# A third early query tile, weight tiles 9 to 11 in halves, and reordered first attention steps in a two-layer decoder trunk

## The reference, cut to what matters

```python
for l in range(DEPTH):                                   # DEPTH = 2
    mod = (silu(c) @ w_ada[l] + b_ada[l])                # 6 vectors of 2048: sh1, sc1, g1, sh2, sc2, g2
    h = rmsnorm(x, norm_g[l, 0]) * (1.0 + sc1) + sh1
    proj = h @ w_in[l]                                   # u | q | kc vc | ks vs | kw vw | gate logits
    a_out = pool_mixer(u, w_pool[l], pool_scale[l])      # trailing means of 2, 4, 8, 16 tokens, mixed
    o_out = nsa_mixer(q, kc, vc, ks, vs, kw, vw, gl, ...)# 8 heads of 128; compressed, selected and window branch
    x = x + g1 * (concat([a_out, o_out]) @ w_out[l])
    h2 = rmsnorm(x, norm_g[l, 1]) * (1.0 + sc2) + sh2
    gate, up = split(h2 @ w_gate_up[l])
    x = x + g2 * ((silu(gate) * up) @ w_down[l])
```

## Time and profile before

| | |
|---|---|
| median of three runs | 2164.11 us (2162.68 to 2164.99) |
| the profiled execution: time, span | 2160.73 us, 2158.9 us |
| busy in the span: PE, weight loads of PE, DVE, ACT, POOL | 98%, 78%, 72%, 45%, 10% |
| chain that ended last, by engine | PE 90%, DMA 4%, DVE 3%, issue 1%, ACT 1% |
| PE's waits in total, largest | 19.2 us of ACT's x_sb L1447 in four, 11.2 the longest |
| HBM read | 592.18 MB, 275 GB/s over the span |

### The profile page before, as it was taken

One profiled execution on the slowest core, in us unless ns is written; L12 is line 12 of the kernel. 1 busy time (PEld: TensorE's weight loads), 2 busy tenths in 40 slices (PEclk: granted clock), 3 DMA queues, 4 the chain that ended last, 5 costly groups with the idle time before them and its releaser, 6 DMA issues.

```text
span 2158.9 us, 25242 instructions
## 1 busy us (share of the span) xinstructions
PE 2125.4 (98%) x9600; PEld 1681.6 (78%) x9600; DVE 1547.0 (72%) x2267; ACT 978.9 (45%) x1509; POOL 208.4 (10%) x392
## 2 busy tenths in 40 slices
PE   7989999999999999999999999999999999999999
PEld 3445788788888888888878788878888888888887
DVE  6776999898688887787877775678755555455555
ACT  2123664744344434444465476475434443344443
POOL 3211222111011111111101100001000000000000
PEclk9999999999999999999999999999999999999999
DMA  9999999899598888888757864468755555555554
GB/s 394 412 376 352 368 345 383 327 350 356 205 346 315 323 320 320 312 320 320 294 196 278 324 251 184 156 233 309 287 214 195 190 184 193 194 191 188 189 192 156
DMA packets 112028, 595.97 MB, mean 276 GB/s; under 512 B 12642, under 2 KB 13090, under 8 KB 65188
## 3 DMA queue, kind: packets, MB, share of 16 engines
q1 hardware_dynamic: 55232, 390.83, 48.5%
q0 software_dynamic: 56384, 203.45, 25.3%
q10 hardware_dynamic: 292, 0.09, 0.0%
HBM read 592.18 MB, written 2.13 MB: 275 GB/s over the span
## 4 chain that ended last, share of the span: by engine, by line
PE 90%; DMA 4%; DVE 3%; issue 1%; ACT 1%; SPq 0%; DVEq 0%; ACTq 0%
PE ps L679 78%; PE ps L787 2%; DMA pT<-w_ada 1%; PE ps L936 1%; PE ps L1095 1%; PE ps L1200 1%; PE ps L1064 1%; PE ps L649 1%; PE ps L642 1%; PE ps L648 1%; DMA ada<-w_ada 1%; DMA raw<-stream 1%; DMA uc<-w_ada 1%; DVE ada L1771 1%; PE ps L1141 1%
## 5 line engine op out<-in xcount | busy, mean ns | idle before, releaser
L1741 DVE TENSOR_TENSOR w_lo<-raw,w_hi 128x1024 fp32r<-128x1024 f32 x658 | 791.1, 1222 | 325.4 <-ACT w_hi L1321 324.8
L1321 ACT ACTIVATE w_hi<-raw 128x1024 fp32r<-128x1024 f32 x658 | 688.2, 1057 | 635.8 <-PE ps L679 611.3
L679 PE MATMUL ps<-w_hi,h_hi 128*128 128x512 f32 x1672 | 458.7, 396 | 0.0
L679 PE MATMUL ps<-w_hi,h_lo 128*128 128x512 f32 x1672 | 447.8, 390 | 0.0
L679 PE MATMUL ps<-w_lo,h_hi 128*128 128x512 f32 x1672 | 447.6, 389 | 0.0
L679 PEld LDWEIGHTS ps<-w_hi,h_lo 128*128 128x128 f32 x1672 | 313.8, 188 | 66.4
L679 PEld LDWEIGHTS ps<-w_lo,h_hi 128*128 128x128 f32 x1672 | 313.9, 188 | 66.2
L679 PEld LDWEIGHTS ps<-w_hi,h_hi 128*128 128x128 f32 x1672 | 309.3, 188 | 64.9 <-issue 4.0
L679 PE MATMUL ps<-w_hi,a_hi 128*128 128x512 f32 x848 | 234.4, 398 | 0.0
L679 PE MATMUL ps<-w_hi,a_lo 128*128 128x512 f32 x848 | 227.0, 389 | 0.0
L679 PE MATMUL ps<-w_lo,a_hi 128*128 128x512 f32 x848 | 226.9, 389 | 0.0
(11 more groups left out here) (251 smaller groups left out, 1625.4 us busy)
## 6 DMA issues: line engine op xcount, KB each, us to landing
raw<-stream SPq DMA_DIRECT2D x358, 1024.0 KB, 5.4
ada<-w_ada POOLq DMA_DIRECT2D x186, 512.0 KB, 6.8
qT<-w_ada POOLq DMA_DIRECT2D x56, 512.0 KB, 7.3
uc<-w_ada POOLq DMA_DIRECT2D x30, 512.0 KB, 7.4
kT<-w_ada POOLq DMA_DIRECT2D x27, 512.0 KB, 7.4
val<-w_ada POOLq DMA_DIRECT2D x27, 512.0 KB, 8.5
pT<-w_ada POOLq DMA_DIRECT2D x27, 512.0 KB, 7.2
gate<-w_ada POOLq DMA_DIRECT2D x16, 512.0 KB, 7.6
```

The source lines that it names most:

```text
L679: mm = pe.matmul(banks[tok][0][:], rows[2 * a + k][low][:, tok * P:(tok + 1) * P], w[s][:, k, :], start=first and a == 0 and i == 0 and k ...
L1321: act.activation(whi[h % 4][:].rearrange("p k c -> p (k c)"), raw[t % 4][:, a * 1024:(a + 1) * 1024], ACT.Copy).then_inc(hi_ready.sem, 1)
L1741: dve.tensor_tensor(wlo[h % 4][:].rearrange("p k c -> p (k c)"), raw[t % 4][:, a * 1024:(a + 1) * 1024], whi[h % 4][:].rearrange("p k c -> ...
```

## The change

- `Q1_EARLY` becomes (22, 23, 20): tile 20 too is loaded to the buffer `gate`, behind tile 9 on SP and once `q1_used` is 2, and PE does it in `first_chunks` ahead of the seventh pair, the blocks (12,13). It leaves the stream buffers and `first_queries`. GpSimd's loads into `gate` and ACT's copy of the early sums wait for the third use instead of the second.
- Tiles 9, 10 and 11 come in two halves each: the first halves (blocks 12 and 13) where the whole tiles were loaded, the three second halves in a row behind the first half of tile 11 and after the 55th w_ada sum. The seventh pair waits for the first halves only, block 14 for the whole tiles.
- In `first_queries` tile 25 follows `hidden(3)`, with `hidden_fold` in its middle, then `cmp_out`, then the two transposes of the first query half.
- The new `first_pooling` runs tiles 26 and 27 of layer 0: `scores(0)` moves to the middle of tile 26, step 26 behind tile 26, `kcmp_turn`, and step 27 with the compressed scores to the middle of tile 27.
- DVE's `add_parts` moves to the front of period 25 and waits for the transposes of the first query half too.

```diff
--- before.py
+++ after.py
@@ -63,7 +63,8 @@
 
 UNSPLIT = half_of(T_SPLIT)
 RAW_AFTER = {1: 6, 2: 8, 3: 12, 9: 44, 12: 62}
-Q1_GROUPS, Q1_EARLY, EARLY_BEHIND = (2, 0, 1, 3), (22, 23), 8
+T_HALVED, HALVES_AFTER = (9, 10, 11), 55
+Q1_GROUPS, Q1_EARLY, EARLY_BEHIND = (2, 0, 1, 3), (22, 23, 20), 8
 HALVES = half_of(TILES)
 PART_HALVES = 2 * PART_TILES
 assert HALVES % 4 == 0
@@ -416,6 +417,7 @@
         bank_b = Bank(ps[6], count("b_full", b_uses, 3), count("b_free", b_uses, 3, 1))
 
         raw_landed = [count(f"raw_landed{s}", 4 * TILES, 4 * PART_TILES) for s in range(4)]
+        half_landed = [count(f"half_landed{t}") for t in T_HALVED]
         raw_free = [count(f"raw_free{s}", TILES // 4, PART_TILES // 4) for s in range(4)]
         ada_first = [count(f"ada_first{s}") for s in range(ADA_SLOTS)]
         ada_landed = {s: count(f"ada_landed{s}") for s in sorted({s for s, _, _ in ADA_SLOT[FIRST_HALVES:]})}
@@ -496,7 +498,7 @@
             def load_early(i):
                 if i:
 
-                    sp.wait_ge(q1_used.sem, 1)
+                    sp.wait_ge(q1_used.sem, i)
                 else:
                     sp.wait_ge(ada_summed.sem, 4)
                 sp.dma_start(gate[:], flat[Q1_EARLY[i]]).then_inc(q1_landed.sem, 16)
@@ -520,6 +522,14 @@
                 elif n >= 4:
 
                     sp.wait_ge(raw_free[s].sem, n // 4)
+                if n in T_HALVED:
+                    sp.dma_start(raw[s][:, 0:1024], flat[n, :, 0:1024]).then_inc(half_landed[n - T_HALVED[0]].sem, 16)
+                    if n == T_HALVED[-1]:
+                        sp.wait_ge(ada_summed.sem, HALVES_AFTER)
+                        for t in T_HALVED:
+                            sp.dma_start(raw[t % 4][:, 1024:2048], flat[t, :, 1024:2048])\
+                                .then_inc(raw_landed[t % 4].sem, 16)
+                    return
                 sp.dma_start(raw[s][:, 0:cols], flat[n, :, 0:cols]).then_inc(raw_landed[s].sem, 16)
 
             def spread_gate(layer, n):
@@ -544,6 +554,8 @@
                         load(layer * TILES + t + 4)
                     if layer == 0 and t + 4 == EARLY_BEHIND:
                         load_early(1)
+                    if layer == 0 and t + 4 == EARLY_BEHIND + 1:
+                        load_early(2)
                     for d in FREED_LATE.get(t, ()):
                         load(layer * TILES + d + 4)
                     if t in GATE_AT:
@@ -574,7 +586,7 @@
                 if before is not None:
                     pool.wait_ge(ada_summed.sem, before + 1)
                 elif s in (9, 10):
-                    pool.wait_ge(q1_used.sem, 2)
+                    pool.wait_ge(q1_used.sem, 3)
                 pool.dma_start(ada_buf[s], w_ada[q]).then_inc(ada_landed[s].sem, 16)
 
             here = Place()
@@ -789,7 +801,7 @@
                                            start=(kt == 4 * first), stop=(kt == KT - 1))
                         if t == T_Q1[3] and (a, tok) == (0, 0):
 
-                            mm.then_inc(gemm_done.sem, 9)
+                            mm.then_inc(gemm_done.sem, 13)
                         elif a == 0 or g == 3:
                             mm.then_inc(gemm_done.sem, 1)
                         elif tok == 0:
@@ -880,7 +892,7 @@
                     for i in range(4):
                         mm = pe.matmul(bank.tile[:], xT[:, 4 * h + i, tok * P:(tok + 1) * P],
                                        gate[:, i * COLS:(i + 1) * COLS],
-                                       start=(h == 0 and i == 0), stop=(h == 1 and i == 3))
+                                       start=(h == 0 and i == 0), stop=(h == 2 and i == 3))
                 mm.then_inc(q1_used.sem, 1)
 
             def skip_landed(t):
@@ -899,6 +911,7 @@
                 hidden(0)
                 q0(15)
                 kv_turn(2)
+                skip_landed(T_CMP1[1])
                 hidden(1)
                 q0(17)
                 skip_landed(T_CMP1[2])
@@ -906,22 +919,33 @@
                 skip_landed(T_Q0[3])
                 q0(18)
                 hidden(3)
-                unsplit(T_Q1[0], chunk(C_Q + 1), Q1_GROUPS[0], lambda: None, Q1_GROUPS[0])
-                hidden_fold()
+                unsplit(T_Q1[3], chunk(C_Q + 1), Q1_GROUPS[3], hidden_fold, Q1_GROUPS[3])
+                cmp_out()
                 stage_turn(bank_a, A_USE["q 0"], ST_Q0, 0, 4)
                 stage_turn(bank_b, B_USE["q 0"], ST_Q0 + 1, 1, 4)
-                unsplit(T_Q1[3], chunk(C_Q + 1), Q1_GROUPS[3], lambda: attention_side(25), Q1_GROUPS[0])
-                cmp_out()
+
+            def first_pooling():
+
+                def steps():
+                    attention_side(27)
+                    middle(27)
+
+                unsplit(26, chunk(C_U), 0, lambda: attention_side(25))
+                attention_side(26)
+                kcmp_turn()
+                unsplit(27, chunk(C_U), 1, steps)
 
             def first_chunks(chunks):
 
                 steps = [(2 * p, 2 * p + 1) for p in range(7)] + [(KT - 2,), (KT - 1,)]
                 for ks in steps:
-                    if ks[0] in (6, 10):
-                        early_queries((ks[0] - 6) // 4)
+                    if ks[0] in (6, 10, 12):
+                        early_queries((6, 10, 12).index(ks[0]))
                     for i, banks in enumerate(chunks):
                         t = T_KV + KV_CHUNKS * (ks[0] // 4) + i
-                        if ks[0] % 4 == 0:
+                        if ks[0] % 4 == 0 and t in T_HALVED:
+                            pe.wait_ge(half_landed[t - T_HALVED[0]].sem, 16)
+                        elif ks[0] % 4 == 0 or (ks[0] == KT - 2 and t in T_HALVED):
                             loaded(t)
                         if ks[-1] == KT - 1 and i == 2:
                             kv_turn(0)
@@ -1007,7 +1031,7 @@
                                    raw[t % 4][:, j * P:(j + 1) * P],
                                    start=(pos < 4), stop=(pos >= CMP_LEN - 4))
                 if piece < 3:
-                    mm.then_inc(raw_free[t % 4].sem, 2 if here.layer == 0 and piece == 2 else 1)
+                    mm.then_inc(raw_free[t % 4].sem, 2 if here.layer == 0 and piece in (1, 2) else 1)
                 else:
                     mm.then_inc(bank_m.full.sem, 1)
 
@@ -1266,7 +1290,11 @@
                         hidden(2)
                     if t == 20:
                         hidden(3)
+                if layer == 0:
+                    first_pooling()
                 for i, t in enumerate((*range(T_U0, T_U0 + 4), *T_U1)):
+                    if layer == 0 and t < T_U0 + 2:
+                        continue
                     if t == 27:
                         kcmp_turn()
                     attention_side(t)
@@ -1450,7 +1478,7 @@
                     act.activation(h_hi[:, 2 * p:2 * p + 2, :].rearrange("p k t -> p (k t)"),
                                    xT[:, 2 * p:2 * p + 2, :].rearrange("p k t -> p (k t)"), ACT.Copy)\
                         .then_inc(norm_hi.sem, 1)
-                act.wait_ge(q1_used.sem, 2)
+                act.wait_ge(q1_used.sem, 3)
                 act.wait_ge(ada_summed.sem, QUERIES_FREE)
                 for tok, bank in enumerate((bank_a, bank_b)):
                     act.activation(q1_part[tok], bank.tile[:], ACT.Copy).then_inc(q1_kept.sem, 1)
@@ -1957,6 +1985,8 @@
                 for tok in range(TOKS):
                     b = chunk_bank(C_Q + 1, tok)
                     dve.wait_ge(gemm_done.sem, gemm_done.at(here, 2 * half_of(T_Q1[3]) + 2 + tok + 1))
+                    turned, use = ((bank_a, A_USE), (bank_b, B_USE))[tok]
+                    dve.wait_ge(turned.full.sem, turned.full.at(here, use["q 0"] + 1))
                     dve.tensor_tensor(bufb[:, tok, :], ps[b][:], q1_part[tok], ALU.add)\
                         .then_inc(chunk_free[b].sem, 1)
 
@@ -2158,6 +2188,8 @@
 
             def period(t, nxt):
                 m = STEP_PERIODS.index(t) if t in STEP_PERIODS else -1
+                if t == 25 and here.layer == 0:
+                    add_parts()
                 if 0 <= m < NSTEP:
                     bias(m)
                 for u in range(4):
@@ -2191,8 +2223,6 @@
                     stage_scale(4)
                 if t == 23:
                     silu_hidden()
-                if t == 25 and here.layer == 0:
-                    add_parts()
                 if t == 25:
                     take_cmp()
                 if t == 27:
```

## The result

The changed kernel takes 2169.75 us (2168.63 to 2176.74) beside 2164.11 us (2160.48 to 2169.11) for the kernel before, seven runs each: ratio 1.0036, 95% interval 1.0023 to 1.0050. It is slower, by 5 to 11 us by the interval. The two medians differ by 5.6 us; the ratio stands for 7.8. The profiled execution took 2172.53 us with a span of 2170.7; a second profile of the same kernel has a span of 2165.1, so one profile stands for its time only within some us.

A forecast was written before the change was run, and what follows sets the result against it. It took PE, 98% busy, as the bound, but DVE and ACT from 195.77 to 232.96 us. PE's 1.5 us lead gave nothing there; the late attention step added 4.6 us to 2164.1, forecast 2168.7 us, range 2162.4 to 2172.5.

The forecast's parts named there:

- Tile 20 in the gap: Ahead of the pair (12,13): tile 20 fills PE's 5.68 us gap, the clock stays up, transposes at 139.3.
- The halves at 0: Tiles 9 to 11 loaded in halves: two more PE waits and three more SP issues, costed at 0.
- part 1: Early loads on SP's queue: tile 20 adds 1 MB, the halves take out 1.5 MB, about the same traffic for w_ada.
- Tile 21's wait goes: In `first_queries`: with tile 20 gone, tile 21 lands in time and PE's 1.22 us wait goes.
- Tile 25: Behind `hidden(3)`: its buffer is released late, so PE waits 5.3 us for the load, plus 1.3 us of slow clock.
- Rival B: Tile 25's load takes 9.2 us instead of 4.7: +9.1 us, 2173.2; chance 0.15.
- The price of the clock: Behind the gap at tile 25: PE's fall to 1.2 GHz costs 1.3 us.
- A2: At tile 25's gap PE keeps 2.4 GHz and the 1.3 us go: +3.3 us, 2167.4; chance 0.17.
- PE's lead of 1.5 us: At tile 25, slow clock included: PE at 184.4 where the kernel before, without fold and transposes, would be at 185.90.
- step 3: Tile 21: PE's wait of 1.22 us goes and `hidden(3)` starts at 176.64.
- step 4: Tile 25's load after `hidden(3)`: a PE gap of 5.3 us and 1.3 us of slow clock.
- `scores(0)` late, chain without slack: First attention step: `scores(0)` at 197.1, 6.5 us later; `take_cmp` 4.6 us later, carried over DVE and ACT to 233.

The follow-up runs named there:

- experiment 6: The halves of tiles 9 to 11 alone, added to the kernel before, tile 20 left where it was: 2158.30 us, ratio 0.9985 to the kernel before.
- experiment 7: The changed kernel with tiles 9 to 11 loaded whole again, tile 20 still ahead of the seventh pair: 2172.87 us, ratio 1.0056 to the kernel before.
- experiment 3: The changed kernel with tile 25 loaded early to tile 20's old buffer and `scores(0)` right behind tile 25: 2160.30 us, ratio 0.9990 to the kernel before.
- experiment 4: The changed kernel with `scores(0)` right behind tile 25, tile 25's buffer and wait kept: 2167.07 us, ratio 1.0023 to the kernel before.
- experiment 1: The changed kernel measured once more, also called the repeat: 2170.79 us, ratio 1.0039 to the kernel before.
- experiment 2: The changed kernel with tile 25 loaded early to tile 20's old buffer, tile 24 behind `hidden(3)`: 2163.41 us, ratio 1.0008 to the kernel before.
- experiment 5: The changed kernel with six dummy products on PE ahead of tile 25: 2167.90 us, ratio 1.0025 to the kernel before.

## Why the prediction was right, and where not

The sign and the range held. The size was short: +4.6 us of 2164.1 is a ratio of 1.0021, just under the interval's 1.0023 and well under the 1.0036 and 1.0039 measured. That the forecast time of 2168.7 lies within about 1 us of the median of 2169.75 is partly luck: the medians differ by 5.6 us where the ratio has 7.8, and two of the terms below were short.

1. *Tile 20 in the gap*: held. Early queries took 7.03, the clock stayed at 1.00, the transposes came at 139.64 for a forecast 139.3, and tile 20 landed in 8.9 us, between the 7.9 and 11.7 of the earlier trace rows. The sentence that the w_ada pieces meet about the same traffic held too (118.07 against 118.21).
2. *The halves at 0*: mis-sized, as a part of the change. Nothing of them was late, as said (they went out at 115.73; the 114.2 of the prediction has no row behind it), but they are worth -3.2 us alone and about -4 in the change (experiments 6 and 7). I asked only what they cost PE. The traffic was in my own count of part 1, 1.5 MB out and 1 MB in, and I netted the two instead of pricing each. The sum came out right since both errors cancel, and the forecast told nothing of which half of the change was good.
3. *Tile 21's wait goes*: held. But 0.55 us at tile 17 and 0.64 ahead of `hidden(2)` took its place, and `hidden(3)` started at 178.43, not 176.64. Both waits are in the second profile of the kernel before as well (0.34 and 0.66), so they are not shown to come from the change.
4. *Tile 25*: held in its cause and size, 5.21 and 5.84 us for a forecast 5.3. Rival B, 9.2 us for the load, is out; the chain shows 5.07. The price of the clock was mis-sized: I took 1.3 us, and the half behind the gap took 2.7 and 1.6 us too long in two profiles (6.34 and 5.16 against 3.60). A2 is out with it. The rule of the Trainium skill that a PE left idle on a DMA falls back to 1.2 GHz (TensorE: Matmul & The Clock Gate, HAM oscillation) has the trace on its side: 0.50 behind the gap of 5.21 us, 1.00 where dummy products filled it. The Trainium skill also says that DMA engines take turns between the queues with work (DMA: Bandwidth & Descriptors, Queues, rings and completion order). That did not make this load late, 5.07 us against 9.2; it agrees with experiment 6, where the share of GpSimd's queue is 88.1% without tile 20 on SP's queue and 74.6% with it.
5. *PE's lead of 1.5 us*: did not come. Tile 25's second half began at 191.04 before and begins at 191.33 here. The transposes (0.91) and `scores(0)` (0.43) lay ahead of it before and don't now, so PE is 0.29 + 0.91 + 0.43 = 1.6 us behind instead of 1.5 ahead. The 1.8 us of step 3 and 1.4 of clock in step 4 make this 3.2.
6. *`scores(0)` late, chain without slack*: held, and it is the step that experiments 3 and 4 test. It came at 200.32 for 197.1, which is again the 3.2 us. `take_cmp` was 7.7 us late in this profile for a forecast 4.6 (whose own terms, 200.3 less 195.77, give 4.5), and nearly all of it was still there at the chain's end (7.6). The product there came at 240.56 for a forecast of about 237.6. In the repeat it came at 238.59.

From the chain's end on, a clock of 0.50 at 242 to 244, after PE's wait of 1.87 us, cost the first profile another 1.7 us, which the prediction had not: PE took 43.0 us from 240.56 to the gate logits' turn at 283.56, where the kernel before took 41.3 (232.96 to 274.28) and the repeat 41.3 (238.59 to 279.93). Why one execution has it and another not stays open.

The budget of the whole change, by ratios: halves -3.2 us (0.9985); gap, clock and late `scores(0)` together +10.6 (1.0039 - 0.9990). These make +7.4, against 7.8 and 8.4 measured. What is left for tile 20 in the old gap can't be told from nothing: experiment 3 has it and the halves (0.9990), experiment 6 the halves alone (0.9985), and their intervals overlap. Both beat the kernel before, by 2.2 and 3.2 us, and the changed one by 10 to 12. The new places of the steps 26 and 27 and of `add_parts` are in every variant of the change and were not measured alone.

## What to carry to other kernels

Work moved into a gap that waits on a full DMA brings its own load. If those bytes go ahead of what the gap waits for, the gap moves back, here by about 5 us for 1 MB. Postponing bytes that weren't needed yet (1.5 MB here) closed the same gap without moving any work. When an edit has two halves with opposite traffic, price each alone before netting them. And work moved away may have been the cover of a load: look up which buffer the next tile takes, and who holds it.

## What was not expected of the hardware

- PE's clock fell to 0.50 (1.2 GHz) not only behind the gaps of 5 us. In the first profile of the changed kernel it fell after the wait of 2.17 us ahead of 207.17, and the half tile at 207.65 took 5.07 us for 3.60. It fell again after a wait of 1.87 us at 240.56:

```profile
240.00:242.00 2.00, 1.45 (x3) 0.80 (x4) 2.00 (x5) 2.00 (x6) 0.69 (x2) 0.83 1.04 424
242.00:244.00 2.00, 2.00 (x4) 0.87 (x4) 1.00 (x3) 1.47 (x2) 0.90 (x2) 0.50 1.04 428
```

  Six other profiles of the changed kernel and its variants have a wait of 1.86 to 1.89 us at that product: in experiments 3 and 7 the clock fell behind it too (0.60 in the window), in experiments 1, 2, 4 and 5 it stayed at 1.00. This slow running is most of the 4.7 us by which PE is busier in the first profile.
- The same gap cost 2.7 us of slow clock in one execution (5.21 us long) and 1.6 in the next (5.84 us). The windows show where the difference lies: in the first the clock was still at 0.91 on average from 180 to 184, while PE was idle, and at 0.50 when it worked. In the second it was low while PE was idle, and back at 1.00 by 188:

```profile
180.00:184.00 4.00, 0.00 (x0) 0.00 (x0) 3.86 (x9) 0.00 (x0) 0.47 (x1) 0.52 0.87 300
184.00:188.00 4.00, 4.00 (x6) 1.87 (x7) 1.65 (x4) 0.00 (x0) 1.12 (x3) 0.63 1.00 406
188.00:192.00 4.00, 4.00 (x13) 1.97 (x12) 1.22 (x4) 0.22 (x1) 0.00 (x0) 1.00 1.00 413
```

- With all DMA engines full, 1 MB more or 1.5 MB less on SP's queue moved the sums of the w_ada pieces, which come by GpSimd's queue, by about 5 us, though the two have queues of their own (experiments 6 and 7).
